# Third program's state space stage: ScalarE makes the convolutions' first product, and the square sums of the gated norm become columns that TensorE spreads over the partitions

## What is computed

```python
def causal_depthwise_conv_3(x, w, bias):          # k_w = 4
    xp = jnp.pad(x, ((0, 0), (k_w - 1, 0), (0, 0)))
    return sum(xp[:, k:k + L] * w[k] for k in range(k_w)) + bias

def gated_group_rmsnorm(y, z, w):                 # 4 groups of 256 channels
    g = y * jax.nn.silu(z)
    g = g.reshape(b, l, SSD_GROUPS, NORM_GROUP)
    g = g * lax.rsqrt(jnp.mean(g * g, axis=-1, keepdims=True) + EPS)
    return g.reshape(b, l, d) * w

def ssd_branch(xBC, dt_raw, z, conv_w, conv_b, dt_bias, A_log, Dh, norm_w):
    xBC = jax.nn.silu(causal_depthwise_conv_3(xBC, conv_w, conv_b))
    ...
    y = ssd_chunked(xs, dt, A, Bm, Cm) + Dh[:, None] * xs
    return gated_group_rmsnorm(y, z, norm_w)
```

## Time and profile before

| | us |
|---|---|
| median of 3 runs | 3282.16 (3276.44 to 3284.37) |
| profiled execution, its own time | 3279.56 |
| its span | 3277.7 |
| PE busy | 3116.9 (95% of the span) |
| DVE busy | 1689.8 (52%) |
| ACT busy | 1129.9 (34%) |
| POOL busy | 955.3 (29%) |

### The profile page before, as it was taken

How to read it: one execution, slowest core, us unless ns; L and a number is a source line. 1 busy time by engine, 2 the same in 40 slices (tenths; PEclk the granted TensorE clock), 3 DMA queues, 4 the chain that set the end, 5 groups by cost and what they waited for, 6 DMA issues and landing times.

```text
span 3277.7 us, 38033 instructions
## 1 busy us (share of the span) xinstructions
PE 3116.9 (95%) x15348; PEld 2444.3 (75%) x15348; DVE 1689.8 (52%) x2730; ACT 1129.9 (34%) x1910; POOL 955.3 (29%) x699
## 2 busy tenths in 40 slices
PE   8999989999989999999999978899999899999998
PEld 6776667666878888777887755687777688788876
DVE  6979651112546644243333467667667745543435
ACT  2125543112441121113331275444445422322334
POOL 4211001112417784125421112321011123442522
PEclk9999989999999999999999989999999999999999
DMA  4110001112312332114331101331011145433322
GB/s 125 51 32 20 14 14 45 39 52 109 130 58 82 90 115 76 45 48 145 112 94 33 39 27 52 116 98 33 26 46 46 36 125 125 133 135 109 103 71 102
DMA packets 251055, 242.22 MB, mean 74 GB/s; under 512 B 15360, under 2 KB 198016, under 8 KB 249856
## 3 DMA queue, kind: packets, MB, share of 16 engines
q1 hardware_dynamic: 228944, 195.52, 19.5%
q10 hardware_dynamic: 21936, 44.27, 3.9%
HBM read 201.03 MB, written 38.73 MB: 73 GB/s over the span
## 4 chain that ended last, share of the span: by engine, by line
PE 80%; DVE 8%; ACT 5%; DMA 2%; POOL 2%; issue 2%; SPq 1%; ACTq 0%; DVEq 0%
PE psum L539 21%; PE psum L541 21%; PE psum L540 21%; PE psum L657 3%; PE psum L545 3%; DMA arena<-in_w_in 2%; DVE arena L2792 1%; PE psum L703 1%; PE psum L729 1%; PE psum L1159 1%; PE psum L840 1%; PE psum L1110 1%; POOL WS L3070 1%; PE psum L1109 1%; DVE arena L2673 1%
## 5 line engine op out<-in xcount | busy, mean ns | idle before, releaser
L3070 POOL TENSOR_TENSOR WS<-arena,WS 128x1024 fp32r<-128x1024 f32 x271 | 673.8, 2492 | 1862.6 <-ACT WS L1175 1862.4
L539 PE MATMUL psum<-XH,WS 128*128 128x512 f32 x2464 | 986.4, 400 | 34.2 <-POOL XL L3126 15.6
L541 PE MATMUL psum<-XH,WS 128*128 128x512 f32 x2464 | 963.1, 391 | 0.0
L540 PE MATMUL psum<-XL,WS 128*128 128x512 f32 x2464 | 962.8, 391 | 0.0
L539 PEld LDWEIGHTS psum<-XH,WS 128*128 128x128 f32 x2464 | 464.6, 189 | 149.7 <-issue 30.1
L541 PEld LDWEIGHTS psum<-XH,WS 128*128 128x128 f32 x2464 | 464.5, 188 | 99.0
L540 PEld LDWEIGHTS psum<-XL,WS 128*128 128x128 f32 x2464 | 465.0, 189 | 96.3 <-issue 4.8
L1175 ACT ACTIVATE WS<-arena 128x1024 fp32r<-128x1024 f32 x271 | 284.7, 1059 | 677.5 <-PE psum L541 243.2
L539 PE MATMUL psum<-WS,XH 128*128 128x512 f32 (+1 forms) x1024 | 396.0, 387 | 19.4 <-DVE XL L2108 7.2
L540 PE MATMUL psum<-WS,XH 128*128 128x512 f32 (+1 forms) x1024 | 392.9, 384 | 0.0
L541 PE MATMUL psum<-WS,XL 128*128 128x512 f32 (+1 forms) x1024 | 392.5, 383 | 0.0
(11 more groups left out here) (291 smaller groups left out, 3257.9 us busy)
## 6 DMA issues: line engine op xcount, KB each, us to landing
arena<-in_w_in SPq DMA_DIRECT2D x85, 512.0 KB, 3.7
arena<-in_w_out SPq DMA_DIRECT2D x48, 512.0 KB, 3.3
arena<-in_w_in_even SPq DMA_DIRECT2D x48, 512.0 KB, 4.1
arena<-in_w_out_even SPq DMA_DIRECT2D x32, 512.0 KB, 3.2
h_spill<-arena ACTq DMA_DIRECT2D x24, 512.0 KB, 3.1
arena<-s_table SPq DMA_DIRECT2D x8, 1536.0 KB, 6.8
arena<-in_w_in_odd SPq DMA_DIRECT2D x18, 512.0 KB, 3.7
s_table<-arena SPq DMA_DIRECT2D x32, 256.0 KB, 3.0
```

The lines of the kernel that those rows point to most:

```text
L539: e.matmul(ps, wh, xh, start=start, stop=False)
L540: e.matmul(ps, wh, xl, start=False, stop=False)
L541: return e.matmul(ps, wl, xh, start=False, stop=stop)
L3070: e.tensor_tensor(lo, raw(book.raw_of.get(("w", u), 0), kbs, n), hi.bitcast(F32), SUB).then_inc(*w.up("w_lo", u))
```

## The change

Two things are changed in the stage.

First, in `prep` of the groups 1 to 3 ACT copies the product to RAW3 as before (event `cv_in`), copies the three leading columns itself (`cv_ptail`), and makes the first product with the bias as an Identity activation with scale and bias (`cv_raw`). DVE is left with the three taps. The convolutions of group 0 stay as they are, but for a DVE memset of three columns (`cv_zero`).

Second, the square sum has the squares as weights and one column of ones as the moving operand: 8 matmuls of 128x1 that put the sums of 512 positions on 128 partitions x 4 columns. Scaling, root and reciprocal are 128x4. A new step `row` then has TensorE spread the four columns over all partitions (4 matmuls of 128x128 against the identity), and DVE multiplies from PSUM. `norm` is split in `root` and `row`, the places of the steps are new, the sums move to the bank `sb`, the rows have bank 2 for themselves, and products are left with banks 0 and 1.

```diff
             def prep(g):
                 for i in range(4):
+                    cb, dst = prep_blocks(g)[i]
+
                     def raw_ev(_, half):
+
+                        R = RAW3[half]
                         w.wait_ge("cv_ps", g, i, 0, half)
...
+                        w.wait_ge("cv_c", *((g, i - 1) if i else (g - 1, 3)), half)
+                        e.activation(R[:, 3:515], ps_of("cv_ps", g, i, 0, half), ACT.Copy).then_inc(
+                            *w.up("cv_in", g, i, half))
+                        w.own()
                         if half:
...
+                            e.activation(R[:, 0:3], RAW3[0][:, 512:515], ACT.Copy).then_inc(*w.up("cv_ptail", g, i))
+                            w.own()
                         else:
...
+                            w.wait_ge("cv_zero")
+                        if g >= 2:
+                            w.wait_ge("yo", g - 2, 7)
+                        e.activation(dst[:, half_of(half)], R[:, 0:512], ACT.Identity, bias=col("conv_b_3", cb),
+                                     scale=col("conv_w_3", cb)).then_inc(*w.up("cv_raw", g, i, half))
...
-            pbk = Banks(free_bank, [0, 1, 2])
+            pbk, yb = Banks(free_bank, [0, 1]), Banks(free_bank, [2])
...
-            def step(name, g, half, ring=pbk):
+            def step(name, g, half, ring=None):
                 if name == "sum":
-                    bank = take(ring, ("y_ms", g, half), ("y_v", g, half))
+                    bank = take(ring or sb, ("y_ms", g, half), ("y_v", g, half))
                     for m in range(2):
                         w.wait_ge("y_sq", g, half, m)
-                        t = e.matmul(psum[:, bank, :], ones, SQB[half][m], start=m == 0, stop=m == 1)
+                        for j in range(4):
+                            t = e.matmul(psum[:, bank, j:j + 1], SQB[half][m][:, tile_of(j)], ones[:, 0:1],
+                                         start=m + j == 0, stop=m + j == 4)
                     t.then_inc(*w.up("y_ms", g, half))
+                elif name == "row":
+                    bank = take(ring or yb, ("y_row", g, half), ("y_nrm", g, half))
+                    w.wait_ge("y_rc", g, half)
+                    for j in range(4):
+                        t = e.matmul(psum[:, bank, tile_of(j)], YR[half][:, j:j + 1].broadcast_to([128, 128]), ident,
+                                     start=True, stop=True)
+                    t.then_inc(*w.up("y_row", g, half))
...
-            for name, half in (("gate", 0), ("sum", 0), ("gate", 1), ("norm", 0), ("sum", 1), ("norm", 1)):
+            for name, half in (("gate", 0), ("sum", 0), ("gate", 1), ("root", 0), ("sum", 1), ("row", 0), ("root", 1),
+                               ("row", 1)):
...
-                     beside(chain(prep(2), zg(1, 0), zg(1, 1)), gate_order(step, 0), (2, 3, 4, 5, 6, 7)),
+                     beside(chain(prep(2), zg(1, 0), zg(1, 1)), gate_order(step, 0), (1, 2, 2, 3, 3, 4, 4, 5)),
...
+                if e_ == 1:
+                    step("row", 3, 1, Banks(free_bank, [6]))
```

More of the change, by code:

```diff
@@ L44 @@
     "ch_dve": "ch_f ch_b ch_s0",
-    "y_dve": "y_gate y_v y_rc y_nr",
+    "y_dve": "cv_zero y_gate y_v y_rc y_nr",
     "s5_dve": "h5_z uc_v ug_v s5v yt",
@@ L440, in last_half @@
         def last_half(step):
-            for name in ("gate", "sum", "norm"):
+            for name in ("gate", "sum", "root", "row"):
                 step(name, 3, 0)
@@ L1863, in step @@
                             *w.up("y_sq", g, half, m))
-                elif name == "norm":
+                elif name == "sum":
                     w.wait_ge("y_v", g, half)
-                    e.activation(SQB[half][0], SQB[half][0], ACT.Sqrt).then_inc(*w.up("y_rt", g, half))
+                    e.activation(YR[half], YR[half], ACT.Sqrt).then_inc(*w.up("y_rt", g, half))
             def load_t(e_):
@@ L1951, in scalar_program @@
             for e_ in range(7):
-                uproj(e_ + 1, e_, lambda: e_ or step("norm", 3, 1))
+                uproj(e_ + 1, e_, lambda: e_ or step("sum", 3, 1))
                 if e_ == 0:
@@ L2774, in dt_add, with taps @@
                                     *w.up("dt_add", half))
+            def taps(g, i, half, R):
+                cb, dst = prep_blocks(g)[i]
+                o = dst[:, half_of(half)]
+                w.wait_ge("cv_raw", g, i, half)
+                for k in range(1, 4):
+                    w.own()
+                    e.scalar_tensor_tensor(o, R[:, k:k + 512], col("conv_w_3", 16 * k + cb), o, M, A_).then_inc(
+                        *w.up("cv_k", g, i, half, k, also=[("cv_c", g, i, half)] if k == 3 else []))
             def conv(g, i, half, R, before):
                 cb, dst = prep_blocks(g)[i]
-                cw = [col("conv_w_3", 16 * k + cb) for k in range(4)]
-                o = dst[:, half_of(half)]
                 w.wait_ge("cv_raw", g, i, half)
@@ L2786, in conv @@
                 w.own()
-                if g >= 2:
-                    w.wait_ge("yo", g - 2, 7)
-                e.tensor_scalar(o, R[:, 0:512], cw[0], col("conv_b_3", cb), M, A_).then_inc(*w.up("cv_k", g, i, half, 0))
-                for k in range(1, 4):
-                    w.own()
-                    e.scalar_tensor_tensor(o, R[:, k:k + 512], cw[k], o, M, A_).then_inc(
-                        *w.up("cv_k", g, i, half, k, also=[("cv_c", g, i, half)] if k == 3 else []))
+                e.tensor_scalar(dst[:, half_of(half)], R[:, 0:512], col("conv_w_3", cb), col("conv_b_3", cb), M, A_).then_inc(
+                    *w.up("cv_k", g, i, half, 0))
+                taps(g, i, half, R)
             def conv_first(n):
@@ L2823, in prep @@
                 for i in range(4):
-                    yield from proj_cm(1, lambda _, half: conv(g, i, half, RAW3[half], RAW3[0]))
+                    yield from proj_cm(1, lambda _, half: taps(g, i, half, RAW3[half]))
             def before(g, c):
@@ L2979, in vector_program @@
             mid(0, scanned=lambda: step("sum", 3, 1))
-            step("norm", 3, 1)
+            step("root", 3, 1)
+            step("row", 3, 1)
             for e_ in range(7):
```

28 lines of the change are left out of this document (13 added, 15 removed).

## The result

The changed kernel takes 3273.06 us (median of 9 runs, 3271.06 to 3277.27); the kernel before took 3284.37 (9 runs, 3276.44 to 3289.22). The ratio is 0.9969, with a 95% interval of 0.9960 to 0.9977: 10.2 us faster by the ratio, 11.3 by the medians, about 0.3%. The profiled execution, which was the fastest of the nine, has a span of 3269.3 us and 3271.06 us of its own time, against 3277.7 and 3279.56.

A forecast was written before the change was run, and what follows sets the result against it. PE, busy 95% of the span, was taken as the bound, waiting mainly for DVE. Terms -3.6 - 1.7 - 1.7 - 8.3 + 1.0 = -14.3 on 3279.56 give 3265.3; with the median 2.6 above, 3268 us, range 3252 to 3281.

The forecast's parts named there:

- new waits on bank 6: Groups 1 and 2: sum waits for the state update, state matmul for scaled sums; 2.1, 2.8 and 1.3 us in group 1.
- group 0: Convolutions only, no norm: PE is the bound afterwards; shorter first wait, less slow clock and faster pairs of turns, -3.6 us.
- group 1: Convolutions and norm: less slow clock and two late reciprocals gone pay for the rows, waits remain 7 us; -1.7 us.
- group 2: Taken to go like group 1, with the same waits and gains; -1.7 us.
- group 3: Norm without convolutions: -2.6 us in the turns, 4.9 at the last wait, 0.8 of slow matmuls; -8.3 us.
- S5, rest: Behind the stage, the last half's sum and row go on PE, which is never idle there; +1.0 us.
- About 1.3 us of the first wait, as much of its slow clock: Group 0: gained at PE's first wait, with 0.3 to 0.7 us a pair of turns besides, for -3.6 us together.
- hold by POOL: In a first half the first tap is held until POOL ends, so DVE gains some 0.5 us, not 2.0.
- rival (b): PE runs free: first taps not held, 3 us of new waits go in groups 1 and 2; -24, 3258 us; chance 0.20.
- rival (c): Dearer new waits, slow sums and clock: groups 1 and 2 +2.5 us each, -6 in all, 3276 us; chance 0.19.
- (d): Slower: close norm steps lengthen turns 1 to 3 in groups 1 and 2; +9 to +10, 3292 us; chance 0.07.
- 4.9 more: End of group 3: gain in us at PE's 7.0 us wait, after a 0.9 us row and a 1.5 us wait.

The follow-up runs named there:

- e8: The changed kernel with a plain ScalarE copy in place of the first product, leaving out weight and bias of the first tap; 3271.32 us.
- e6: e3 with the eight norm steps of groups 1 and 2 at the places of the kernel before (turns 2, 3, 4, 5, 6, 6, 7, 7); 3294.36 us.
- e7: e3 with the eight norm steps of groups 1 and 2 at turns 1, 2, 3, 3, 4, 4, 5, 5; 3287.10 us.
- e3: The changed kernel with the columns of the sums in bank 2 instead of bank 6; 3265.98 us, ratio to the kernel before 0.9945.
- e1: The kernel before with only the first product of the convolutions of groups 1 to 3 moved to ScalarE, norm as before; 3280.45 us, ratio 0.9988.
- e2: The kernel before with only the norm's part of the change, its places and banks, first product still on VectorE; 3275.83 us, ratio 0.9975.
- e9: e3 with group 3's row of half 0 in bank 7 and groups 1 and 2's steps at 1, 2, 3, 3, 4, 5, 5, 6; 3260.74 us.
- e10: e3 with the row of half 0 of group 3 in bank 7, the same kernel as e5, five runs; 3263.82 us, ratio to before 0.9938.
- e4: The changed kernel with the first product of the second halves back on VectorE; 3270.38 us, ratio to the kernel before 0.9955.
- e5: e3 with the row of half 0 of group 3 in bank 7 instead of bank 2, one run; 3262.14 us.

## Why the prediction was right, and where it was off

Forecast was 3268 us, in a range of 3252 to 3281; measured was 3273.06. 2.2 of the 5.1 us are the kernel before itself, whose median was 3282.16 in the first 3 runs and 3284.37 in all 9. The mechanism was the forecast one: new waits on bank 6 take back much of what VectorE gives. Term by term, against the differences of the rows above:

```
            forecast  measured
group 0       -3.6      -2.30
group 1       -1.7      -1.01
group 2       -1.7      -2.35
group 3       -8.3      -7.49
S5, rest      +1.0      +2.7
```

Ahead of the stage the changed kernel's trace is 2.1 us longer; nothing was changed there, and the two traces of the kernel before differ there by 4.8. Of the signs that the prediction names, PE's idle time fell to 15.1 us (about 18 forecast), the sum waited for the state update once a group (1.85 and 1.91 us), and the lanes' transposes waited 1.95 us (1 to 2).

**Group 0 was mis-sized, and its step was "About 1.3 us of the first wait, as much of its slow clock".** PE before, and then in the changed kernel, one L991 for each turn:

```profile
2226.89 0.49 PE L989 MATMUL psum<-arena 128*128 128x128 f32 x2 [1.92 <-DVE arena L2856]
```

```profile
2228.07 0.49 PE L991 MATMUL psum<-arena 128*128 128x128 f32 x2 [0.81 <-DVE arena L2884]
2237.78 0.49 PE L991 MATMUL psum<-arena 128*128 128x128 f32 x2 [0.80 <-DVE arena L2884]
2246.55 0.38 PE L991 MATMUL psum<-arena 128*128 128x128 f32 x2
2255.18 0.38 PE L991 MATMUL psum<-arena 128*128 128x128 f32 x2
2263.80 0.38 PE L991 MATMUL psum<-arena 128*128 128x128 f32 x2
```

The first wait fell by 1.1 us, but one of 0.80 stands in the next turn, where there was none. The two turns with the waits took 17.6 us instead of 19.3 (L991 and L989 from 2220.21 and 2217.92 on), a gain of 1.7 where the working had 2.6. The turns behind gave 0.8 more, where it had 1.0, and 0.2 were lost ahead of the first. So the pairs of turns were sized about right, although "PE's own two turns are 2 x (3.04 + 5.44) = 17.0" was short: a turn of PE is 8.63 us, two are 17.26, since a product takes 5.58 from its first matmul to what follows it and not 5.44; before, a pair took 17.7. That PE is the bound there is confirmed by e8: a ScalarE operation shorter by 184 ns changed group 0 by 0.13 us, and the two waits of 0.8 stayed. Taking 0.63 us for that operation from the earlier trace rows was wrong as well (0.815), and harmless in this group. What causes the wait in the second turn was not tried.

**The hold by POOL is there, and smaller than in the earlier trace rows.** Three taps that nothing holds, three whose first is held, and the POOL instruction that holds it:

```profile
2319.82 2.33 DVE L2806 SCALAR_TENSOR_TENSOR arena<-arena 128x512 f32<-128x512 f32 x3 [2.30 <-ACT arena L1839]
...
2331.25 3.12 DVE L2806 SCALAR_TENSOR_TENSOR arena<-arena 128x512 f32<-128x512 f32 x3 [2.30 <-ACT arena L1839]
```

```profile
2329.89 2.35 POOL L3100 TENSOR_TENSOR WS<-arena,WS 128x1024 fp32r<-128x1024 f32 x1 [19.48 <-ACT WS L1188]
```

The three are 0.8 us longer, all of it in the first (1.55 us instead of 0.75); it starts at 2331.25 and POOL ends at 2332.24. That is what the Trainium skill's page "SBUF — State Buffer", section "Who interferes with whom", says of such a pair: a DVE instruction with two SBUF inputs contends with a GpSimd instruction that reads SBUF, and issue order decides who blocks. The trace agrees: POOL started at 2329.89, ahead of the tap. With it DVE's two turns in group 0 are 9.74 and 6.67 us long (the working had 9.8 and 6.7). The part of rival (b) by which the first taps are free did not come.

**Group 1 went as worked out, wait by wait; that the two groups together give the forecast -3.4 is luck.** PE in group 1 and, behind the dots at the end, in group 2, in order of time:

```profile
2328.48 1.95 PE L1043 MATMUL psum<-arena 128*128 128x1 f32 x16 [1.85 <-DVE arena L2894]
...
2334.49 1.22 PE L1009 MATMUL psum<-arena 128*128 128x256 f32 x2 [2.38 <-DVE arena L2925]
...
2348.13 0.70 PE L1009 MATMUL psum<-arena 128*128 128x256 f32 x2 [1.11 <-DVE arena L2925]
...
2434.03 3.53 PE L1043 MATMUL psum<-arena 128*128 128x1 f32 x16 [1.91 <-DVE arena L2894]
...
2452.33 0.70 PE L1009 MATMUL psum<-arena 128*128 128x256 f32 x2 [1.03 <-DVE arena L2925]
```

Forecast for the first three were 2.1, 2.8 and 1.3 us. DVE's fronts came at 2324.54, 2338.30, 2350.26 and 2361.41, where the working had 2324.9, 2338.6, 2350.3. The rows cost 0.9 us each, 1.05 with the last one's tail. The group's last state matmul runs at 2384.17, where the working had 2383.7: turns of 8.63 us and not 8.5. That leaves 1.3 of the 1.7 us, and 0.2 more go because the group already starts earlier.

Group 2 was taken to be "alike", and that step failed: it gave 2.35. The kernel before has waits there that group 1 does not have (2.77 us at the last L1007 against 1.92, and one more of 1.55 at L989), so more was to be had; and the change costs it other things. The sum ran once at the lower clock, 3.53 us instead of 1.95 (the upper bound was 3.4), and then the scaling was ready and L1009 did not wait: rival (c)'s price was real in one place. The sign "3 to 6 us a group" at L1009 holds in group 1 (3.5) and not in group 2 (1.0).

Rival (c) as a whole needed +2.5 a group and is out; so is (b), since the wait at L1009 is there; and (d), since no group became longer. But e6 and e7 show how near the slow side is: with e3's edit and other places for the steps a group is 11 to 14 us longer than in e3, by waits at the row that the rival did not name.

**What the norm and its banks cost.** The prediction took bank 6 as given with the change. e3 prices that choice: 6.4 us, a third of what both parts can give (19.5).

**Group 3** gave 0.8 less, and all of it at the end. The turns gave 2.7 us (forecast 2.6), and the transposes behind the last wait 0.9 of slow clock (0.8): eight took 1.97 us before and take 1.09 now. The failed term is the "4.9 more" between them, which measured 3.95. The old wait of 7.0 less a row of 0.9 and a wait of 1.5 is 4.6 and not 4.9, and the wait was 1.95. Before:

```profile
2592.41 1.97 PE L545 MATMUL psum<-arena 128*128 128x128 f32 x8 [6.95 <-DVE arena L2912]
```

**S5** took 2.7 us back instead of 1.0, in one trace, and three pieces of it can be told apart. Its first turn, from the first lanes' matmul to the next turn's, has 38.27 us against 37.74 (37.71 in the second trace of before). The sum with the two products behind it takes 12.7 us in both kernels and the row 0.9, near the forecast 1.0; 0.4 come back ahead of them, since the 32 lanes' matmuls and the product behind them are at the higher clock sooner (9.1 us instead of 9.5). e1 has 38.28 without a column or a row, by chance the same: its first product takes 6.44 us where the kernel before has 5.90, at the lower clock for longer behind the same wait. Why it stays there longer is open.

The second turn has 35.73 us against 35.18 and 35.19, and there the product waits for ACT's evacuation, which stands behind a weight:

```profile
2635.27 1.06 ACT L1188 ACTIVATE WS<-arena 128x1024 fp32r<-128x1024 f32 x1 [10.31 <-DMA arena<-in_w_in]
...
2636.86 0.50 PE L541 MATMUL psum<-XH,WS 128*128 128x512 f32 x1 [0.62 <-ACT arena L1908]
```

This is the point named last in the prediction: a weight that arrives later relative to PE (ACT takes it up 51.2 us behind the stage's end, 50.2 before, where no product waits). It costs 0.6 us here, and e1, e2, e3, e8, e9 and e10 have the same wait with 0.3 to 0.6; e4 has none.

The remaining 1.6 us are in the five turns behind and are open. The six turns behind the first sum to 211.7 us in both traces of before, 213.8 in the changed kernel, and 210.7 to 214.2 in the others, whose code there hardly differs; so how much of it is the change's is not shown.

## What to carry to other kernels

When a small step is added between large ones, ask first which accumulator bank it takes and what stands behind that bank in the order: here sums of 1.7 us in a bank of the main chain cost 6.4 us. Another bank cost nothing at these places, and 5.4 us a time at e7's, where a row in the same bank stood directly behind a sum. Where TensorE needs what VectorE makes for a small step, leave a turn between them: in the same turn VectorE's operation stands behind the taps, and these wait for TensorE's own product, so the spread waits 4 to 5 us. And measure a change in its own stage: two traces of one kernel agreed there within 0.05 us and differed by 4.8 us elsewhere.

## What the runs showed of the hardware

- ScalarE's 128x512 operation with a scale and a bias of its own for each partition takes 815 ns, a plain copy of the same shape from SBUF 631, a square 634. Whether the scale, the bias or the function costs the 184 ns was not tried.
- An idle time of 1.95 us on TensorE and one of 0.78 us had 32 small matmuls behind them at the lower clock (3.51 us); idle times of 0.63 and 1.02 us left them at the higher one (1.97 us). The idle time of TensorE thus cost 1.5 us more there than it was long.
- A tap on VectorE that starts while GpSimd reads SBUF takes 1.55 us instead of 0.75; GpSimd's own 2.35 us are not longer than elsewhere (2.41 in the mean before).
- The stage, 424 us on four engines with a dozen waits, repeated within 0.05 us in each group in two traces of the kernel before, and within 0.1 us in the two of e5's kernel. The part ahead of it, the same code in all, varied by 5.5 us over the traces.
